# Attention values with V stationary and probabilities moving, turned output, and sums of squares by a matmul, in a float32 decoder layer

## The chip, the cores and the metric

The kernel runs on one core of a Trainium2 chip. It is one launch. The metric is the device time of one execution in microseconds (us). The engines are TensorE (PE; its weight loads are listed as PEld), VectorE (DVE), ScalarE (ACT), GpSimd (POOL) and SyncE (SP), which issues most DMAs.

## The reference

One pre-norm decoder layer on x of 256 x 1024, float32. Sixteen heads of 64: the first eight (group 0) are mixer A, causal attention (with 256 positions there is one block, so the block selection falls away); the last eight (group 1) are mixer B, a mixture of three dilated windows, which is one softmax with the log of a position's multiplicity added as a mask. What is computed, cut to what matters:

```python
qkv = jnp.einsum('bsd,de->bse', rmsnorm(x, attn_norm), w_in)
q, k = rope(q), rope(k)
p = softmax(q @ k.T * ATTN_SCALE + mask[group])     # per head
o = p @ v                                            # per head, 64 wide
o_g = rmsnorm(o of group g, 512 wide, gain_g)        # g = 0, 1
x = x + concat(o_0, o_1) @ w_out
h = rmsnorm(x, ffn_norm)
x = x + (silu(h @ w_gate) * (h @ w_up)) @ w_down
return rmsnorm(x, final_norm)
```

## The kernel before

All large matmuls run in three passes: activations and weights are split into a high part (written as fp32r by ACT) and a rest (DVE), and `three_pass` (L403 to L405) adds hi x hi, hi x lo and lo x hi in PSUM. The weights come as blocks of 128 x 512 through a ring of 12 (`raw`, `w_hi`, `w_lo`): SP loads four at a time (`ring_quad`), ACT splits pairs (L636), DVE makes the rest (L831), PE uses them. Blocks 0 to 47 are the q, k and v projections (six outputs in the order of `QKV_ORDER`, eight blocks each, six matmuls per block), 48 to 63 the output projection (four blocks at a time, first for rows 0 to 127, s = 0, then for s = 1), the rest the FFN, of which a loop does most.

Attention is laid between the blocks. Three tables, `PE_PLAN`, `DVE_PLAN` and `ACT_PLAN`, say behind (PE) or before (DVE, ACT) which block number an engine does which item; each engine takes its queue strictly in that order, so an item that waits holds what stands behind it. DVE's and ACT's splits stand in the same queues, behind the items of an odd number. On the items, with g the group and s or half the half of the rows:

- `rope` on DVE, in `rope_a`, `rope_b` and `rot`; `turn` transposes q or k on PE, ACT and DVE split it.
- `score(g, u)`: PE computes the scores of two tiles of 512 columns, the heads of even number on rows 0 to 63 of the array and those of odd number on rows 64 to 127 (L451 to L456), into banks 4 and 5; DVE adds the mask and takes the maxima; ACT does the exponentials with their sums (L720). u = 0 holds the first 128 queries of all eight heads, with 128 keys; u = 1 and 2 the other queries of four heads each, with 256 keys.
- `squares(g, t)`: DVE transposes the probabilities of tile t in squares of 32 (L921); SP places the squares by 4 DMAs into `landed` (`place_probs`, L368); `place` on ACT copies `landed` into `probsT` with its columns in order (L738).
- `values(g, t)`: PE, with a head's transposed probabilities stationary (128 x 128) and the head's 64 columns of `vals` moving, into bank 7 (L471), queries on the partitions.
- `norm`: DVE takes the reciprocal of the sums (L928) and multiplies bank 7 by it into `o_sb` (L931). `oturn`: PE transposes `o_sb` into bank 6 (L481); ACT squares `o_sb` with an accumulated sum (L667) and writes `o_hi` from bank 6 with the gain (L730); `olo` on DVE writes the rest (L941).
- `residual` on DVE adds a finished half of the output projection, scaled by rstd, which POOL makes for each group and half from the sum of squares.

## Time and profile before

| What | us |
|---|---|
| Median of 3 runs | 311.64 (311.19 to 312.02) |
| The profiled execution | 311.84 |
| Its span in the trace | 309.9 |
| PE busy, share of the span | 301.3, 97% |
| DVE busy | 200.7, 65% |
| ACT busy | 170.8, 55% |
| POOL busy | 10.3, 3% |
| DMA, mean share of 16 engines | 56.2% weights, placings and the like |

The span is what the trace covers; what lies around it is 1.9 us. Matmuls are pipelined and overlap in the records, so one that is listed with 390 ns comes every 230 ns; the distance of starts, or the pieces of the chain, tell what an instruction costs the engine. A float32 matmul appears as two instructions, an fp32r one as one. A group's mean is taken over its records.

### The profile page before, as it was taken

How to read it: one execution, taken by the hardware profiler on the slowest of the kernel's cores; microseconds unless marked ns; L12 is line 12 of the kernel's file. 1: busy time of each engine (PE TensorE's matmuls, PEld its weight loads, DVE VectorE, ACT ScalarE, POOL GpSimd, SP SyncE). 2: the span in 40 equal slices, each digit the busy share in tenths (PEclk: the TensorE clock that was granted, in tenths of full speed). 3: DMA queues.
4: the chain of work that ended last, by engine and by line, in shares of the span. 5: the costliest groups of instructions: out<-in, count | busy, mean ns of one | idle time of the engine just before them, and what ended most of it. 6: DMA issues, size and time to landing. Idle time of an engine off the chain costs nothing.

```text
span 309.9 us, 4293 instructions
## 1 busy us (share of the span) xinstructions
PE 301.3 (97%) x1430; PEld 246.1 (79%) x1430; DVE 200.7 (65%) x323; ACT 170.8 (55%) x294; POOL 10.3 (3%) x24
## 2 busy tenths in 40 slices
PE   7999999999999999999999999999999999999991
PEld 3788877788888988888888888888888888888880
DVE  3677979997877388855757374656565555555425
ACT  4785563968678458746453443526354444444224
POOL 0001000000020020200000000000000000000002
PEclk9999999999999999999999999999999999999998
DMA  6997635568482355482985656565657474561003
GB/s 200 390 410 298 222 111 161 189 185 286 116 285 71 144 170 237 153 316 78 347 326 170 224 183 210 187 223 176 252 170 270 161 256 174 209 220 31 0 0 135
DMA packets 22332, 61.59 MB, mean 199 GB/s; under 512 B 2608, under 2 KB 14000, under 8 KB 16432
## 3 DMA queue, kind: packets, MB, share of 16 engines
q1 hardware_dynamic: 22032, 60.89, 56.2%
q10 hardware_dynamic: 288, 0.54, 0.5%
q8 instruction: 7, 0.11, 0.1%
q14 instruction: 5, 0.04, 0.0%
HBM read 54.60 MB, written 1.05 MB: 180 GB/s over the span
## 4 chain that ended last, share of the span: by engine, by line
PE 96%; DMA 1%; ACT 1%; DVE 0%; POOLq 0%; issue 0%; POOL 0%
PE bank L403 30%; PE bank L404 29%; PE bank L405 29%; PE bank L471 3%; PE bank L430 2%; DMA gain<-in_gains 1%; PE bank L451 1%; PE bank L481 1%; PE bank L454 1%; PE bank L413 1%; PE bank L455 0%; PE bank L456 0%; POOLq L193 0%; ACT junk L667 0%; ACT rot L811 0%; DVE w_lo L851 0%
## 5 line engine op out<-in xcount | busy, mean ns | idle before, releaser
L636 ACT ACTIVATE w_hi<-raw 128x1024 fp32r<-128x1024 f32 x94 | 97.9, 1057 | 81.8 <-PE bank L405 71.9
L831 DVE TENSOR_TENSOR w_lo<-raw,w_hi 128x1024 fp32r<-128x1024 f32 x94 | 111.8, 1214 | 18.8 <-ACT w_hi L636 17.3
L403 PE MATMUL bank<-w_hi,x_hi 128*128 128x512 f32 x272 | 109.0, 401 | 0.8 <-DVE w_lo L851 0.8
L404 PE MATMUL bank<-w_lo,x_hi 128*128 128x512 f32 x272 | 106.6, 392 | 0.0
L405 PE MATMUL bank<-w_hi,x_lo 128*128 128x512 f32 x272 | 106.5, 392 | 0.0
L403 PEld LDWEIGHTS bank<-w_hi,x_hi 128*128 128x128 f32 x272 | 51.5, 189 | 13.1 <-DVE w_lo L851 2.2
L405 PEld LDWEIGHTS bank<-w_hi,x_lo 128*128 128x128 f32 x272 | 51.5, 189 | 11.1
L404 PEld LDWEIGHTS bank<-w_lo,x_hi 128*128 128x128 f32 x272 | 51.6, 190 | 10.1
L403 PE MATMUL bank<-w_hi,h_hi 128*128 128x512 f32 x80 | 31.2, 390 | 0.0
L405 PE MATMUL bank<-w_hi,h_lo 128*128 128x512 f32 x80 | 31.1, 389 | 0.0
L404 PE MATMUL bank<-w_lo,h_hi 128*128 128x512 f32 x80 | 31.1, 389 | 0.0
L969 DVE SCALAR_TENSOR_TENSOR rope_a<-bank,rstd,rope_b 128x256 f32<-128x256 f32 x22 | 9.8, 480 | 30.3 <-ACT rope_b L762 30.3
L983 DVE TENSOR_TENSOR h_lo<-landed,h_hi 128x512 fp32r<-128x512 f32 x10 | 6.9, 692 | 23.3 <-ACT h_hi L767 23.3
L720 ACT ACTIVATE probs<-probs,neg_max 128x128 f32<-128x128 f32 (+1 forms) x32 | 14.2, 444 | 8.3 <-DVE neg_max L910 8.3
L405 PEld LDWEIGHTS bank<-w_hi,h_lo 128*128 128x128 f32 x80 | 15.0, 188 | 3.1
L403 PEld LDWEIGHTS bank<-w_hi,h_hi 128*128 128x128 f32 x80 | 15.0, 188 | 3.1
L404 PEld LDWEIGHTS bank<-w_lo,h_hi 128*128 128x128 f32 x80 | 15.0, 188 | 3.0
L403 PE MATMUL bank<-w_hi,o_hi 128*128 128x512 f32 x40 | 16.3, 408 | 0.0
L405 PE MATMUL bank<-w_hi,o_lo 128*128 128x512 f32 x40 | 15.7, 392 | 0.0
L404 PE MATMUL bank<-w_lo,o_hi 128*128 128x512 f32 x40 | 15.6, 389 | 0.0
L762 ACT ACTIVATE rope_b<-bank,rstd 128x256 f32<-128x256 f32 x22 | 9.6, 465 | 4.1 <-PE bank L405 4.1
L471 PEld LDWEIGHTS bank<-vals,probsT 128*128 128x128 f32 x96 | 11.5, 192 | 0.4
(75 smaller groups left out, 233.9 us busy)
## 6 DMA issues: line engine op xcount, KB each, us to landing
raw<-in_weights SPq DMA_DIRECT2D x46, 1024.0 KB, 4.8
landed<-p_squares SPq DMA_DIRECT2D x88, 64.0 KB, 2.1
raw<-in_weights SPq DMA_DIRECT2D x5, 512.0 KB, 9.1
o_sb<-in_x_turned SPq DMA_DIRECT2D x4, 256.0 KB, 7.0
xs<-in_x SPq DMA_DIRECT2D x2, 512.0 KB, 8.5
out<-rot SPq DMA_DIRECT2D x4, 256.0 KB, 2.0
raw<-in_weights SPq DMA_DIRECT2D x2, 256.0 KB, 4.1
vals<-in_final_norm ACTq DMA_DIRECT2D x1, 512.0 KB, 7.2
```

Source lines behind the costliest of these rows:

```text
L403: pe.matmul(dst, a_hi, w1, start=first, stop=False)
L404: pe.matmul(dst, a_hi, w2, start=False, stop=False)
L405: return pe.matmul(dst, a_lo, w1, start=False, stop=last)
L413: ins = pe.transpose(dst[:, a * SEQ + s * P:a * SEQ + (s + 1) * P], xs[:, s, kt * P:(kt + 1) * P], ident)
L430: ins = pe.transpose(bank[TURN_BANK[qk_i][s]][:, p * P:(p + 1) * P], rot[:, qk_i, s, p * P:(p + 1) * P], ident_ja if qk_i else ident)
L471: ins = pe.matmul(bank[7][:, head * HEAD_DIM:(head + 1) * HEAD_DIM], probsT[:, T % PT_SLOTS, at:at + P], vals[:, g, b, head * HEAD_DIM:(he ...
L636: act.activation(w_hi[:, slot:slot + 2, :], raw[:, slot:slot + 2, :], ACT.Copy).then_inc(hi_ready, 1)
L720: ins = act.activation(piece, piece, ACT.Exp, bias=neg_max[:, g, half, head:head + 1], scale=-1.0, accum_out=sums[:, g, half, head:head + 1])
L762: act.activation(silu[:, s, :], bank[4 + s][:, 0:FC], ACT.Silu, scale=rstd[:, 6 + s:7 + s]).then_inc(silu_done, 1)
L831: dve.tensor_tensor(w_lo[:, slot:slot + 2, :], raw[:, slot:slot + 2, :], w_hi[:, slot:slot + 2, :].bitcast(f32), ALU.subtract).then_inc(lo ...
L969: dve.scalar_tensor_tensor(hid[:, s, :], bank[4 + s][:, FC:2 * FC], rstd[:, 6 + s:7 + s], silu[:, s, :], ALU.mult, ALU.mult).then_inc(hid_ ...
L983: dve.tensor_tensor(hidden[1], placed, hidden[0].bitcast(f32), ALU.subtract).then_inc(ht_lo, 1)
```

## The change

The values matmuls trade operands. Stationary is now a head's 128 x 64 of `vals`; moving are the 128 columns of its transposed probabilities, read straight from `landed` (four runs of 32 columns). Heads of even number go to the lower 64 columns of the array and lower 64 partitions of bank 7, those of odd number to the upper, alternately. So o comes out transposed, with (head, d) on the partitions and queries in the columns; `place` and `probsT` go, `landed` has 6 slots instead of 3, and three `values` items of 16 instructions stand for each group.

The reciprocal sums now must be transposed too: POOL widens them to 64 columns per head (`widen_rsums`, 512 columns, into `rope_a` or `rope_b`), PE transposes them (`rsum`) and ACT copies them to SBUF, all before `norm`, which multiplies the two. `oturn` goes; `o_hi` and `o_lo` are made from `o_sb`. Since the features are now on partitions, ACT squares `o_sb` (without a sum), POOL adds the four pieces of 128 columns (`add_squares`), and PE sums over the partitions by a matmul with a column of ones (`osum`), once for both halves of a group; DVE scales it, POOL makes rstd, one per group. The reciprocals are a DVE item of their own. The three tables and SP's places (`PLACE`) are written anew; of them two places stand below.

PE, before, from the block ahead of score(1, 0) on (L451 score, L471 values, L454 score(1, 1), L481 oturn; a row with x3 repeats the one above it):

```order
L451 MATMUL bank<-qkT_first 128x128 [waits max_ready,qk_lo,qk_first]
...
L471 MATMUL bank<-vals,probsT 128x64 [waits v_taken,p_placed]
L471 MATMUL bank<-vals,probsT 128x64 x3
L471 MATMUL bank<-vals,probsT 128x64 [waits p_placed]
...
L454 MATMUL bank<-qkT_hi 128x256 [waits max_ready,qk_lo]
...
L481 MATMUL bank<-tab,o_sb 128x128 [waits qk_lo,o_ready]
...
L471 MATMUL bank<-vals,probsT 128x64 [waits o_ready,p_placed]
```

The same stretch now (L461 score, L487 values, L464 score(1, 1)):

```order
L461 MATMUL bank<-qkT_first 128x128 [waits max_ready,qk_lo,qk_first]
...
L487 MATMUL bank<-landed,vals 64x128 [waits v_taken,rsum_taken,in_p1,in_p0]
L487 MATMUL bank<-landed,vals 64x128 x7
...
L464 MATMUL bank<-qkT_hi 128x256 [waits max_ready,qk_lo]
...
L487 MATMUL bank<-landed,vals 64x128 [waits o_ready,in_p3,in_p2]
...
L487 MATMUL bank<-landed,vals 64x128 [waits in_p5,in_p4]
```

Two `values` items of four matmuls have become one of eight before score(1, 1); the next comes right behind that score and waits for `o_ready`, which the first norm gives; the third stands alone.

ACT, before, from the placings ahead of the exponentials of score(1, 0) to the first o (L698 take, L711 turn, L720 exponentials, L667 and L730 o):

```order
L738 ACTIVATE probsT<-landed 128x512 [waits in_p1]
...
L698 ACTIVATE vals<-bank,rstd 128x512 [waits rstd_ready,blk_done]
...
L711 ACTIVATE qkT_hi<-bank 128x4x128 [waits scored,turned]
L636 ACTIVATE w_hi<-raw 128x1024 [waits blk_done,raw_full0]
L720 ACTIVATE probs,sums<-probs,neg_max 128x128 [waits max_ready]
...
L738 ACTIVATE probsT<-landed 128x512 [waits valued,in_p0]
...
L667 ACTIVATE junk,ssq<-o_sb 128x512 [waits sq_done,o_ready]
L730 ACTIVATE o_hi<-bank,gain 128x128 [waits b6_full]
```

The same stretch now (L738 turn, L756 copy of turned sums, L725 take, L663 splits, L747 exponentials, L763 and L769 o):

```order
L738 ACTIVATE qkT_hi<-qkT_first 128x4x128 [waits qk_first]
L756 ACTIVATE rot<-bank 128x512 [waits turned,rsum_turned]
L738 ACTIVATE qkT_hi<-bank 128x4x128 [waits scored,turned]
L725 ACTIVATE vals<-bank,rstd 128x512 [waits rstd_ready,blk_done]
...
L663 ACTIVATE w_hi<-raw 128x1024 [waits blk_done,raw_full0] x2
L747 ACTIVATE probs,sums<-probs,neg_max 128x128 [waits max_ready]
...
L763 ACTIVATE o_hi<-o_sb,gain 128x128 [waits o_ready]
...
L769 ACTIVATE rot<-o_sb 128x512 [waits turned]
```

The placings are gone, the second copy of turned sums stands ahead of the last turn, one more split stands ahead of the exponentials, and o follows directly on score(1, 0) with its squares last.

The diff, cut to what is spoken of:

```diff
+RSUM_BANK = 7, 6
...
-LANDINGS, PT_SLOTS = 3, 6
+SQUARES, LANDINGS = 3, 6
...
-    41: [("values", 0, 0), ("values", 0, 1)],
-    42: [("score", 1, 1), ("oturn", 0, 0)],
...
+    41: [("values", 0, 0)],
+    43: [("score", 1, 1), ("values", 0, 1)],
...
+        rsums_wide = rope_a, rope_b
+
+        rsums_turned = rot[:, 0, :, :]
+        o_squares, o_halves = rot[:, 1, 0, :], rot[:, 1, 1, 0:SEQ]
+        o_sums = rot[:, 1, 1, SEQ:GW].rearrange("p (s t) -> p s t", s=SH)
...
-                    sp.wait_ge(p_placed, T - LANDINGS + 1)
+                    sp.wait_ge(valued, (T - LANDINGS) // 2 + 1)
                 for i in range(JS):
                     sp.dma_start(landed[:, T % LANDINGS, i, :],
-                                 p_squares[i * SQ:(i + 1) * SQ, T % LANDINGS, :, :]).then_inc(in_p[T % LANDINGS], 16)
+                                 p_squares[i * SQ:(i + 1) * SQ, T % SQUARES, :, :]).then_inc(in_p[T % LANDINGS], 16)
...
                 elif kind == "values":
-                    _, g, t = it
-                    T = g * SC_TILES + t
-                    half, heads, keys = attention_tile(t)
-                    pe.wait_ge(p_placed, T + 1)
-                    if t == 0:
+                    _, g, u = it
+                    half, _, keys = attention_tile(2 * u)
+                    for r in range(2):
+                        T = g * SC_TILES + 2 * u + r
+                        pe.wait_ge(in_p[T % LANDINGS], (T // LANDINGS + 1) * 16 * JS)
+                    if u == 0:
                         pe.wait_ge(v_taken, 2 * g + 2)
-                    if t in (0, 2) and T:
+                        pe.wait_ge(rsum_taken, 2)
+                    if u in (0, 1) and g + u:
                         pe.wait_ge(o_ready, g * 2 + half)
                     kb = keys // P
-                    for i, head in enumerate(heads):
+
+                    for i in range(NB // keys):
                         for b in range(kb):
-                            at = (i * kb + b) * P
-                            ins = pe.matmul(bank[7][:, head * HEAD_DIM:(head + 1) * HEAD_DIM],
-                                            probsT[:, T % PT_SLOTS, at:at + P],
-                                            vals[:, g, b, head * HEAD_DIM:(head + 1) * HEAD_DIM],
-                                            start=(b == 0), stop=(b == kb - 1))
+                            for r in range(2):
+                                T, head = g * SC_TILES + 2 * u + r, attention_tile(2 * u + r)[1][i]
+                                x = i * kb + b
+                                dst = bank[7][64 * r:64 * r + 64, head // 2 * P:(head // 2 + 1) * P]
+                                ins = pe.matmul(dst.rearrange("p (i b) -> p i b", b=SQ),
+                                                vals[:, g, b, head * HEAD_DIM:(head + 1) * HEAD_DIM],
+                                                landed[:, T % LANDINGS, :, x * SQ:(x + 1) * SQ],
+                                                start=(b == 0), stop=(b == kb - 1))
                     ins.then_inc(valued, 1)
-                elif kind == "oturn":
+                elif kind == "rsum":
                     _, g, s = it
-                    pe.wait_ge(o_ready, g * 2 + s + 1)
-                    pe.wait_ge(*((ot_lo, g * 2 + s) if g * 2 + s else (qk_lo, 8)))
-                    for k in range(KT // 2):
-                        ins = pe.transpose(bank[6][:, k * P:(k + 1) * P], o_sb[:, g, s, k * P:(k + 1) * P], ident)
-                    ins.then_inc(b6_full, 1)
+                    n = g * 2 + s
+                    pe.wait_ge(rsum_wide, n + 1)
+                    if n:
+                        pe.wait_ge(rsum_taken, n)
+                    if n == 2:
+                        pe.wait_ge(qk_lo, 8)
+                    for p in range(HPAIRS):
+                        ins = pe.transpose(bank[RSUM_BANK[g]][:, p * P:(p + 1) * P], rsums_wide[s][:, p * P:(p + 1) * P], ident)
+                    ins.then_inc(rsum_turned, 1)
+                elif kind == "osum":
+                    g = it[1]
+                    pe.wait_ge(o_added, g * 2 + 2)
+                    pe.wait_ge(*((o_msq, 1) if g else (max_ready, 2 * SC_TILES)))
+                    for s in range(SH):
+                        ins = pe.matmul(bank[5][:, s:s + 1], o_sums[:, s, :], ones[:, 0:1], start=True, stop=True)
+                    ins.then_inc(o_summed, 1)
...
-                elif kind == "oturn":
+                elif kind == "rsum":
+                    _, g, s = it
+                    act.wait_ge(rsum_turned, g * 2 + s + 1)
+                    act.wait_ge(turned, 6)
+                    if g:
+                        act.wait_ge(o_ready, s + 1)
+                    act.activation(rsums_turned[:, s, :], bank[RSUM_BANK[g]][:], ACT.Copy).then_inc(rsum_taken, 1)
+                elif kind == "o":
                     _, g, s = it
                     n = g * 2 + s
-                    sum_squares(o_sb[:, g, s, :], GW, ssq[:, 2 + n:3 + n])
-                    act.wait_ge(b6_full, n + 1)
+                    act.wait_ge(o_ready, n + 1)
                     for k in range(KT // 2):
                         col = G_MIX + 4 * g + k
-                        ins = act.activation(o_hi[:, g * 4 + k, s * P:(s + 1) * P], bank[6][:, k * P:(k + 1) * P],
+                        ins = act.activation(o_hi[:, g * 4 + k, s * P:(s + 1) * P], o_sb[:, g, s, k * P:(k + 1) * P],
                                              ACT.Copy, scale=gain[:, col:col + 1])
                     ins.then_inc(ot_hi, 1)
-                elif kind == "place":
-                    T = it[1] * SC_TILES + it[2]
-                    act.wait_ge(in_p[T % LANDINGS], (T // LANDINGS + 1) * 16 * JS)
-                    if T >= PT_SLOTS:
-                        act.wait_ge(valued, T - PT_SLOTS + 1)
-                    act.activation(probsT[:, T % PT_SLOTS, :].rearrange("p (x i b) -> p x i b", i=JS, b=SQ),
-                                   landed[:, T % LANDINGS, :, :].rearrange("p i (x b) -> p x i b", b=SQ),
-                                   ACT.Copy).then_inc(p_placed, 1)
+                    if n:
+                        act.wait_ge(o_added, n)
+                    act.wait_ge(turned, 8)
+                    act.activation(o_squares, o_sb[:, g, s, :], ACT.Square).then_inc(o_squared, 1)
...
+                elif kind == "rsum":
+                    _, g, half = it
+                    dve.wait_ge(exp_done, g * SC_TILES + (SC_TILES if half else 2))
+                    dve.reciprocal(rsums[:, g, half, :], sums[:, g, half, :]).then_inc(rsum_ready, 1)
                 elif kind == "norm":
                     _, g, half = it
-                    t = SC_TILES - 1 if half else 1
                     n = g * 2 + half
-                    dve.wait_ge(exp_done, g * SC_TILES + t + 1)
-                    dve.reciprocal(rsums[:, g, half, :], sums[:, g, half, :]).then_inc(rsum_ready, 1)
-                    dve.wait_ge(valued, g * SC_TILES + t + 1)
-                    dve.wait_ge(rsum_ready, n + 1)
-                    dve.tensor_tensor(o_sb[:, g, half, :].rearrange("p (h d) -> p h d", h=GH),
-                                      bank[7][:].rearrange("p (h d) -> p h d", h=GH),
-                                      rsums[:, g, half, :].unsqueeze(2).to_broadcast([P, GH, HEAD_DIM]),
+                    dve.wait_ge(rsum_taken, n + 1)
+                    dve.wait_ge(valued, g * 3 + (3 if half else 1))
+                    dve.tensor_tensor(o_sb[:, g, half, :], bank[7][:], rsums_turned[:, half, :],
                                       ALU.mult).then_inc(o_ready, 1)
+                elif kind == "osum":
+                    g = it[1]
+                    dve.wait_ge(o_summed, g + 1)
+                    dve.tensor_scalar(msq[:, 2 + 2 * g:4 + 2 * g], bank[5][:, 0:SH], 1.0 / GW, EPS, ALU.mult,
+                                      ALU.add).then_inc(o_msq, 1)
...
-                        dve.wait_ge(rstd_ready, rstd_count[f"o{g}{s}"])
+                        dve.wait_ge(rstd_ready, rstd_count[f"o{g}"])
...
+            def add_squares(n):
+                pool.wait_ge(o_squared, n + 1)
+                if n >= 2:
+                    pool.wait_ge(o_summed, 1)
+                link(pool.tensor_tensor(o_halves, o_squares[:, 0:SEQ], o_squares[:, SEQ:GW], ALU.add))
+                pool.tensor_tensor(o_sums[:, n % 2, :], o_halves[:, 0:P], o_halves[:, P:SEQ],
+                                   ALU.add).then_inc(o_added, 1)
+
+            def inverse_rms_of_o(g):
+                c = slice(2 + 2 * g, 4 + 2 * g)
+                pool.wait_ge(o_msq, g + 1)
+                pool.tensor_tensor(rstd[:, c], msq[:, c], neg_half[:, c], ALU.pow).then_inc(rstd_ready, 1)
+
+            def widen_rsums(n):
+                g, s = n // 2, n % 2
+                pool.wait_ge(rsum_ready, n + 1)
+                pool.wait_ge(*((rsum_turned, n - 1) if g else (rotated, 8)))
+                pool.tensor_copy(rsums_wide[s][:].rearrange("p (h d) -> p h d", h=GH),
+                                 rsums[:, g, s, :].unsqueeze(2).to_broadcast([P, GH, HEAD_DIM])).then_inc(rsum_wide, 1)
+
+            widen_rsums(0)
+            widen_rsums(1)
+            widen_rsums(2)
+            add_squares(0)
+            add_squares(1)
+            widen_rsums(3)
+            inverse_rms_of_o(0)
+            add_squares(2)
+            add_squares(3)
+            inverse_rms_of_o(1)
+            inverse_rms_of_parts((6, 8), 4, 6)
```

## Rows read from the trace of the kernel before

**Rows 1.** The page: busy time by engine; the chain that ended last, by engine.
```profile
PE 301.3 (97%) x1430; PEld 246.1 (79%) x1430; DVE 200.7 (65%) x323; ACT 170.8 (55%) x294; POOL 10.3 (3%) x24
...
PE 96%; DMA 1%; ACT 1%; DVE 0%; POOLq 0%; issue 0%; POOL 0%
```

**Rows 2.** Waits of PE: who waited for whom, total us, times, longest.
```profile
PE bank L529 <- DVE warm L826: 1.2, 1, 1.2
PE bank L403 <- DVE w_lo L851: 0.8, 1, 0.8
```

**Rows 3.** Busy time by stretch: length, PE, PEld, DVE, ACT, POOL, clock, DMA, GB/s.
```profile
60.00:115.00 55.00, 55.00 (x323) 46.26 (x322) 41.29 (x92) 39.63 (x92) 4.58 (x8) 1.00 0.56 181
```

**Rows 4.** The chain in order of time: start us, us, what.
```profile
57.28 0.63 PE bank L430 x4
...
67.93 0.92 PE bank L430 x4
...
73.89 1.09 PE bank L451 x16
74.99 0.43 PE bank L403
75.42 0.23 PE bank L404
...
76.57 1.73 PE bank L471 x16
78.31 0.29 PE bank L403
...
79.75 0.32 PE bank L454 x2
80.66 0.59 PE bank L481 x4
...
82.63 3.52 PE bank L471 x32
...
90.33 0.44 PE bank L481 x4
...
94.66 0.84 PE bank L471 x8
```

**Rows 5.** Timeline of PE and its weight loads: start us, us, engine, line, operation.
```profile
73.82 1.16 PE L451 MATMUL bank<-qkT_first 64*128 64x128 f32 x16
...
76.41 1.89 PE L471 MATMUL bank<-vals,probsT 128*128 128x64 f32 x16
...
76.18 1.98 PEld L471 LDWEIGHTS bank<-vals,probsT 128*128 128x128 f32 x16
```

**Rows 6.** Groups by line and shape: busy us, mean ns | idle before.
```profile
L720 ACT ACTIVATE probs<-probs,neg_max 128x128 f32<-128x128 f32 x16 | 6.2, 389 | 1.1 <-DVE neg_max L910 1.1
...
L451 PE MATMUL bank<-qkT_first 64*128 64x128 f32 x32 | 2.3, 285 | 0.0
```

**Rows 7.** Timeline of ACT ahead of the exponentials of score(1,0).
```profile
72.05 1.25 ACT L698 ACTIVATE vals<-bank,rstd 128x512 f32<-128x512 f32 x2
73.19 0.59 ACT L711 ACTIVATE qkT_hi<-bank 128x512 fp32r<-128x512 f32 x1
74.94 1.06 ACT L636 ACTIVATE w_hi<-raw 128x1024 fp32r<-128x1024 f32 x1 [1.16 <-DMA raw<-in_weights]
```

**Rows 8.** Timeline of DVE: end of the last rope; squares(1,0) and norm(0,0).
```profile
68.15 0.69 DVE L874 TENSOR_TENSOR rot<-rope_a,rope_b 128x512 f32<-128x512 f32 x1
...
78.47 0.70 DVE L921 STREAM_TRANSPOSE p_squares<-probs 128x512 f32<-128x512 f32 x1
...
79.36 0.69 DVE L931 TENSOR_TENSOR o_sb<-bank,rsums 128x512 f32<-128x512 f32 x1
```

**Rows 9.** Timeline of POOL (its longest instruction) and of SP's queue (one placing).
```profile
109.17 1.44 POOL L1055 TENSOR_TENSOR rstd<-msq,neg_half 128x1 f32<-128x1 f32 x1
...
79.20 2.49 SPq L368 DMA_DIRECT2D landed<-p_squares  x4
```

170 lines of the change are left out of this document (87 added, 83 removed).

## Prediction

> **What bounds the kernel now.** First the page [rows 1]: TensorE (PE) is busy for 97% of the 309.9 us span, and 96% of the chain that ended last is PE's. Next whom PE waits for [rows 2]: the whole list is 1.2 + 0.8 us, both before the first weights are split. In the stretch where the values of attention are computed, 60 to 115 us [rows 3], PE is busy for all 55 us, at a granted clock of 1.00, the upper of its two levels. So two things can move the end: how long PE's own instructions take, and any wait that the change brings before one of them. The other engines have room: of the 55 us ACT is busy for 39.6, DVE for 41.3, POOL for 4.6 [rows 3].
>
> I price each thing that PE does between projections as its piece in the chain plus what the next weight matmul (L403) takes above its usual 0.23 us [rows 4].
>
> **Part 1, the values: -3.00 us.** Removed are the 96 L471 instructions (48 matmuls; each float32 matmul runs as two). In the chain they are five pieces, 1.73, 3.52 twice and 0.84 twice, 10.45 us, and the L403 behind each takes 0.05 or 0.06 too much (0.29 at 78.31): 10.74 us [rows 4]. What sets their pace? 16 in 1.73 us is 0.108 us each, and the x32 piece gives 0.110. They move only 64 columns. The L481 transposes move 128 columns in the same time, 0.44 us for 4 [rows 4], so two of these L471 should fit in it if columns were the limit. What both have in common is a load of 128 x 128 [rows 5]: it is the load that paces them.
>
> Added are 96 instructions as well, six items of 16: stationary is now 128 x 64 of vals, moving are 128 columns of landed, alternately into the lower and the upper 64 partitions of bank 7. Ends of their price: if the two halves of the array do not work side by side, each instruction moves 128 columns in 0.11 us (L481), and an item is 1.76 us before any extra for changing over. If they do, the nearest row is L451: also 16 instructions, float32, 128 moving columns, two heads alternately on two halves of the array (there rows 0-63 and 64-127, here columns). It takes 1.09 us, plus 0.20 in the L403 behind it: 1.29 us [rows 4]. Its own pace is 0.058 us each (1.16 us from first start to last end [rows 5], less the 0.285 us that one lasts [rows 6], over 15 steps), about half of 0.11; the rest, some 0.35 us, is paid once per item for going into and out of halves. A load of half as many columns should take half of 0.11, so that two fit beneath one pair's 0.117. I take L451's value, since kind, count, width and alternation agree: 6 x 1.29 = 7.74, and 10.74 - 7.74 = 3.00 us saved. Ends kept: 6 x 1.2 = 7.2 (3.5 saved) and 6 x (16 x 0.11 + 0.35) = 12.7 (2.0 lost).
>
> Do loads run beneath matmuls at all? The L471 rows say so, for matmuls on the very same rows of the array: 16 loads fill 1.98 us from 76.18 on, and 16 matmuls 1.89 us from 76.41 on [rows 5], where one after the other they would need the sum. The Trainium skill, "TensorE: Matmul & The Clock Gate", section "The mechanism", says that a weight load overlaps with matmuls in flight only when its row group differs, and two column halves share all row groups; by it the six items would lose what is priced as rival A, where the rows alone would save 3.0 us.
>
> **Part 2, transposes: 0.** Four items of four o transposes (L481: 0.44 us each, 0.59 beside a score [rows 4]) go; four items of four transposes of the widened inverse sums come, same shape. 4 x 0.44 against 3 x 0.44 + 0.59 is at most 0.15 less; I count nothing.
>
> **Part 3, sums of squares by PE: +0.95 us.** Two items of two float32 matmuls with one moving column: 8 instructions that load 128 x 128. With so few columns the load sets the pace, so L471 is the row: 8 of them are 0.84 + 0.05 us [rows 4], with a little for the second item's edge 0.95. Below it cannot fall much, loads of 128 being what they are; above, 0.35 us per item if narrow matmuls cost like a changeover: 0.9 to 1.6.
>
> **Part 4, the plan: -0.2 us.** The first turn of the second group is 0.63 us in the chain at 57.28, where four transposes of that form cost 0.44 (90.33) [rows 4]: it stands one block behind the score whose maxima it waits for. It now stands three blocks later. Scores and other turns keep number and shape.
>
> **Part 5, waits that could open.** I walked the new order by the old durations; a weight block on PE is 6 x 0.23 = 1.38 us.
> (a) ACT loses 12 placings and gains 4 copies of turned sums, all of 512 columns, so its total falls; o's squares stay, without the 4 readouts. (b) The tightest place: PE's second values item (behind block 43) overwrites bank 7 and waits for o_ready, so for DVE's first norm, and that now stands behind squares(1,0), squares(1,1), hence behind all eight exponentials of score(1,0). Count from the end of that score on PE. ACT's queue in front of the exponentials starts with the copy of the sums that PE turned 1.38 + 1.29 us earlier: the copy about 0.6 (like the turn), turn 0.59, take 1.25, two weight splits of 1.06 [rows 7], is 4.5, so ACT is free at +1.8; eight exponentials of 0.39 [rows 6]: +4.9; transpose, reciprocal and norm took DVE from 78.47 to 80.05 [rows 8], 1.6: +6.5. PE: three blocks 4.1, values 1.29, score(1,1) 0.91 (79.75 to 80.66) + 0.20 [rows 4]: +6.5. A tie. I count +0.15 us; here any lateness of ACT is paid in full by PE, and behind it in the queues stand only later scores and splits, which lead PE by microseconds (the pair for blocks 46 and 47 is split before it). (c) PE's rsum(0,0) waits for POOL to widen the sums, which waits for the last rope on DVE. That ended at 68.8 [rows 8]; a DVE turn and its wait for ACT no longer stand ahead of it, a short reciprocal does, and the walk has it at 67.6. PE comes there after the turn that the chain has at 67.93 for 0.92 us [rows 4], one block later and 0.2 us early: 70.0. So 1.2 us of room by the old time, 2.4 by the walk. No row shows POOL on 512 elements; its dearest instruction is 1.44 us [rows 9], DVE's 128 x 512 take 0.7 [rows 8]. I take 1.3, which the walk's room covers: no cost; at 4 us PE would wait 1.6 us once. (d) rstd for o now comes late: osum on PE, msq on DVE, then POOL; DVE's residual(0) waits with olo(1,0) behind it, which PE needs for block 56. In the walk olo(1,0) ends at 105.8 and PE comes at 108.5: 2.7 us of room, again POOL's. (e) SP: each placing holds its queue for 2.5 us [rows 9], and quads stand behind. Quad (4,1) now goes out behind placing 6, at about 83, and lands near 88; PE needs it at 100. Covered.
>
> The Trainium skill, "GPSIMD Engine Reference", section 3.1, gives a two-input add on POOL 1.96 times DVE's time; 0.7 us would become an estimated 1.4, inside the room in (c) and (d). No row here shows it, and the sum would not change.
>
> **Sum.** -3.00 + 0 + 0.95 - 0.2 + 0.15 = -2.1 us, all on PE. Nothing takes it back later: PE waits for nobody up to the last matmul [rows 2], and the quads that feed it leave SP no later than before. The profiled execution took 311.84 us (span 309.9): 309.7. The median, 311.64, gives 309.5; I say 309.6, and count the rivals from the same middle, 311.7.
>
> **Rivals.**
> A, slower: the halves take turns. Then an item is 16 x 0.11 + 0.35 = 2.1 us instead of 1.29, six are 12.7, and the sum is 1.9 + 0.9 = +2.8: 314.5 us. For: two streams now read the same 128 partitions, where L451's read 64 each. Against: at 128 columns in 0.11 us float32 moves at half the pace of the main matmuls (512 in 0.23 us [rows 4]), which leaves room for a second stream. The end turns to slower from an item of 1.64 us on, (10.74 - 0.9) / 6. A second way into the same place: the loads of the halves do not run beneath matmuls but stand bare, 2 x 0.055 us on top of each pair's 0.117. That makes 8 x 0.23 + 0.35 = 2.2 us an item, +3.3 in all, 315.0 us; as loads do run beneath matmuls in [rows 5] it gets 3 of A's 13 in 100. The rule of the Trainium skill named in part 1 would bring it about.
> B, about the same: the halves overlap, but place (b), (c) or (d) opens by 1 to 2 us. ACT a microsecond behind the walk, or POOL at 4 us or more for 512 elements, would do. Sum -1.1 to -0.1: 311.1 us. Against: all places but one have over 2 us of room.
> C, partly: a pair costs 0.16 to 0.18 us (a load of 64 columns dearer than half of one of 128): an item 1.6 to 1.8, sum -0.1 to +0.9: 312.1 us.
> D, the change frees more than counted (items at 1.2 or under, no tie): sum -2.9: 308.8 us.
>
> **Chances.** Forecast (308.9 to 310.6) 58, B 16, A 13, C 8, D 5 in 100. The range takes in the forecast, D, B and the lower edge of C: 308.4 to 312.0; it leaves out A and most of C. A measurement of this kernel can tell about 0.3%, 0.94 us, from no change. Faster by more: the forecast, D and a quarter of B, 0.67. Within: the rest of B, and C, 0.20. Slower: A, 0.13.
>
> **What would show it.** Values items of 1.1 us in the chain, 16 instructions each at 0.06 us: part 1 right; at 0.11: A. The L403 behind them near 0.43. Two pieces of 0.4 to 0.5 us for the sums. A PE wait on DVE's norm ahead of the second values item: (b), its length the error of the walk. A wait on ACT's copy near 70 or on ot_lo near 106: POOL, with its 128 x 512 copies over 2.3 us. PE busy for all but 2 us of the span up to 301 would mean that nothing was given back.

## The result

| | median, us | lowest to highest |
|---|---|---|
| Kernel before | 311.8 (4 runs) | 311.19 to 312.02 |
| Changed kernel | 308.99 (4 runs) | 308.27 to 309.37 |

The ratio is 0.991, 95% interval 0.9887 to 0.9934: faster by 0.9%, 2.8 us. Timed once more on another chip beside a fresh set of runs of the kernel before, it gave 309.26 us against 311.68, 0.9914 [0.9898, 0.9930]. The prediction was 309.6 us. One execution in all that follows, of runs_contiguous, took 430.8 us at a mean granted clock of 0.66 and is slow; no ratio counts it.

**The profile after.** The profiled execution took 309.37 us, its span is 307.5 us. Busy time by engine, and the chain that ended last, by engine (against [rows 1]):

```profile
PE 297.4 (97%) x1438; PEld 239.8 (78%) x1438; DVE 201.7 (66%) x325; ACT 166.8 (54%) x282; POOL 18.4 (6%) x31
...
PE 93%; DMA 3%; SPq 1%; ACT 1%; DVE 0%; POOLq 0%; issue 0%; POOL 0%
```

PE's busy time fell by 3.9 us, POOL's rose by 8.1. Whom PE waits for: in total us, times, longest (against [rows 2]):

```profile
PE bank L413 <- DVE w_lo L878: 2.5, 3, 1.4
PE bank L556 <- DVE warm L853: 1.2, 1, 1.2
```

All four of these stands end by 14.2 us, at the start of the kernel, while the first weights are being split; in the second profiled execution of the changed kernel they are 2.3 and 1.2 us. No wait on a norm, on ACT's `o_hi` or on a placed tile has come in. The attention stretch (against [rows 3]; columns: length, PE, PEld, DVE, ACT, POOL, clock, DMA, GB/s) says the same: PE is busy for all of it.

```profile
60.00:115.00 55.00, 55.00 (x347) 43.36 (x347) 42.96 (x94) 37.62 (x82) 12.72 (x14) 1.00 0.55 183
```

The chain in order of time (start us, us, what), with the rows that answer to [rows 4]:

```profile
60.44 0.44 PE bank L440 x4
...
70.48 0.44 PE bank L501 x4
...
75.05 1.09 PE bank L461 x16
76.15 0.43 PE bank L413
...
77.73 1.02 PE bank L487 x16
78.76 0.43 PE bank L413
...
82.65 1.02 PE bank L487 x16
...
98.93 0.34 PE bank L508 x4
99.27 0.35 PE bank L413
```

A values item is 1.02 us in the chain with 0.20 to 0.23 us in the L413 behind it; before, its 16 instructions took 1.73 (L471). What each item adds to the distance between the starts of the weight matmuls around it gives a full account (a weight matmul counted with 0.2285 us):

| us on PE | before | after | difference | predicted |
|---|---|---|---|---|
| values, all | 10.79 | 7.27 | -3.52 | -3.00 |
| first turn of group 1 | 0.69 | 0.45 | -0.24 | -0.2 |
| transposes of o; of the widened sums | 1.77 | 1.77 | 0 | 0 |
| sums of squares by PE | - | 0.92 | +0.92 | +0.95 |
| second values item waiting for a norm | - | 0 | 0 | +0.15 |
| all items of attention and the FFN's turns | 27.17 | 24.36 | -2.81 | -2.1 |

Of the six values items five cost 1.24 to 1.26 us each, and the one directly behind score(1, 1) 1.02.

The span fell by 2.4 us only. In this execution PE's first turn came at 30.66 us against 30.19 before, 0.47 later, ahead of everything that the change touches; in the second profiled execution of the changed kernel it came at 30.21, and there the span is 307.1 us, 2.8 less than before.

### The profile page after: what moved, and what is told of

Same layout as the page of the kernel before. It is cut to its first block, busy times and chain, and to the rows that moved or that the text cites. A ratio compares the mean times of both kernels' runs of the same rounds, so it can differ in the third digit from the quotient of the medians.

```text
span 307.5 us, 4312 instructions
## 1 busy us (share of the span) xinstructions
PE 297.4 (97%) x1438; PEld 239.8 (78%) x1438; DVE 201.7 (66%) x325; ACT 166.8 (54%) x282; POOL 18.4 (6%) x31
## 4 chain that ended last, share of the span: by engine, by line
PE 93%; DMA 3%; SPq 1%; ACT 1%; DVE 0%; POOLq 0%; issue 0%; POOL 0%
PE bank L413 29%; PE bank L415 28%; PE bank L414 28%; DMA raw<-in_weights 3%; PE bank L487 2%; PE bank L440 2%; PE bank L461 1%; PE bank L464 1%; PE bank L501 1%; PE bank L423 1%; SPq L344 0%; SPq L334 0%; PE bank L465 0%; POOLq L192 0%; PE bank L466 0%; ACT junk L694 0%
## 5 line engine op out<-in xcount | busy, mean ns | idle before, releaser
L663 ACT ACTIVATE w_hi<-raw 128x1024 fp32r<-128x1024 f32 x94 | 97.9, 1056 | 82.4 <-PE bank L415 72.4
L858 DVE TENSOR_TENSOR w_lo<-raw,w_hi 128x1024 fp32r<-128x1024 f32 x94 | 112.0, 1217 | 17.4 <-ACT w_hi L663 16.2
L413 PE MATMUL bank<-w_hi,x_hi 128*128 128x512 f32 x272 | 108.2, 398 | 2.5 <-DVE w_lo L878 2.5
L413 PEld LDWEIGHTS bank<-w_hi,x_hi 128*128 128x128 f32 x272 | 51.1, 188 | 15.6 <-DVE w_lo L878 4.2
L413 PE MATMUL bank<-w_hi,h_hi 128*128 128x512 f32 x80 | 31.2, 390 | 0.0
L747 ACT ACTIVATE probs<-probs,neg_max 128x128 f32<-128x128 f32 (+1 forms) x32 | 14.1, 448 | 6.2 <-DVE neg_max L937 6.2
L413 PEld LDWEIGHTS bank<-w_hi,h_hi 128*128 128x128 f32 x80 | 15.0, 188 | 3.1
L413 PE MATMUL bank<-w_hi,o_hi 128*128 128x512 f32 x40 | 16.4, 410 | 0.0
```

The source lines that it names most:

```text
L413: pe.matmul(dst, a_hi, w1, start=first, stop=False)
L663: act.activation(w_hi[:, slot:slot + 2, :], raw[:, slot:slot + 2, :], ACT.Copy).then_inc(hi_ready, 1)
L747: ins = act.activation(piece, piece, ACT.Exp, bias=neg_max[:, g, half, head:head + 1], scale=-1.0, accum_out=sums[:, g, half, head:head + 1])
L858: dve.tensor_tensor(w_lo[:, slot:slot + 2, :], raw[:, slot:slot + 2, :], w_hi[:, slot:slot + 2, :].bitcast(f32), ALU.subtract).then_inc(lo ...
```

## Experiments

The open questions after the result: whether the two halves of the array really work side by side, and what sets the pace; what a visit to the halves costs once, whatever stands in it; how near the waits were that did not come; and where the sums' 0.92 us comes from. "Changed kernel" stands for the 308.99 us (309.26 in the last set).

**halves_in_turn.** Do the halves overlap at all, or are the instructions only short?

```diff
-                    for i in range(NB // keys):
-                        for b in range(kb):
-                            for r in range(2):
+                    for r in range(2):
+                        for i in range(NB // keys):
+                            for b in range(kb):
```

> The changed kernel with one difference: within a values item the eight matmuls of the lower half of the array come first, then the eight of the upper half, instead of alternately. Same instructions, same loads of 64 columns. Theory 1 (the gain of the values comes from two halves at work at the same time): the 16 instructions of an item run at 0.11 us each, as the transposes of 128 columns do, except where the halves meet; an item costs about 1.9 to 2.1 us instead of 1.21, so six add 4.1 to 5.3 us: 313 to 314.5 us. Theory 2 (the gain comes from loads of half the width, and the halves do not matter): the items stay at 1.0 us in the chain and the time at 309.0.

(The eight on each half are instructions; they belong to four matmuls.)

Measured: 311.93 us, ratio 1.0005 [0.9991, 1.0019]: the whole gain is gone. That is less than the 313 to 314.5 us of theory 1, and far from theory 2's 309.0. The chain, and PE's timeline, of an item:

```profile
77.38 1.51 PE bank L487 x16
```
```profile
77.31 1.58 PE L487 MATMUL bank<-landed,vals 128*64 128x128 f32 x16
```

An item costs 1.73 us instead of 1.25 (1.50 behind a score instead of 1.02); 6 x 0.48 = 2.9, which is the difference of the times. The same instructions, in another order: the gain of the change lies in the alternation of the halves. But 1.73 is also less than rival A's 2.1.

**one_half.** Rival A's price itself: in turn, and all in the lower half.

```diff
-                                dst = bank[7][64 * r:64 * r + 64, head // 2 * P:(head // 2 + 1) * P]
+                                dst = bank[7][0:64, head // 2 * P:(head // 2 + 1) * P]
```

> As halves_in_turn, but both sets of eight matmuls go to the lower half of the array and the lower 64 partitions of bank 7 (so the upper heads of o are left wrong). Nothing can run side by side now, while loads stay at 64 columns. Theory 1 (two halves at work at once make the gain; where they met in halves_in_turn about four instructions still ran beside others): 16 x 0.11 us, an item of 1.73 to 2.0 us in all, against 1.21 alternating: +3.1 to +4.7, 312.1 to 313.7 us. Theory 2 (halves_in_turn lost time for another reason than lost overlap): the same 311.9 as there or less.

Measured: 313.94 us, 1.0071 [1.0054, 1.0087]. In the chain:

```profile
77.07 1.89 PE bank L487 x16
```

An item costs 2.10 us, what rival A was priced at (16 x 0.11 + 0.35). Against it halves_in_turn saves 0.38 us per item, where its order meets the other half once: some 3.5 instructions of 0.11 us. That is how far the second half's matmuls ran beside the first half's; it isn't far enough for eight instructions to run beside eight.

The first moments of an item show the two halves directly. PE's timeline of the changed kernel, cut to 77.60 to 77.90 us, and of one_half, cut to 76.95 to 77.20:

```profile
77.66 0.44 PE L487 MATMUL bank<-landed,vals 128*64 128x128 f32 x4
```
```profile
77.00 0.43 PE L487 MATMUL bank<-landed,vals 128*64 128x128 f32 x2
```

In the same time four instructions run alternately and two on one half. In the single records of the changed kernel they start in pairs, under 0.01 us apart, and the pairs come 0.109 us apart behind the first; in one_half single instructions come 0.109 us apart. So each half keeps the pace it has alone, and the 0.0545 us of an alternating instruction is two such streams.

**runs_contiguous.** The moving operand is read as four runs of 32 columns. Does that cost?

```diff
-                                ins = pe.matmul(dst.rearrange("p (i b) -> p i b", b=SQ),
+                                ins = pe.matmul(dst,
...
-                                                landed[:, T % LANDINGS, :, x * SQ:(x + 1) * SQ],
+                                                landed[:, T % LANDINGS, x, :],
```

> The changed kernel, but the values matmuls read 128 contiguous columns of a landed tile instead of four runs of 32 (so they multiply columns in the wrong order; o is left wrong, all else is computed from it as it comes). Theory 1 (runs of 32 columns cost PE nothing): 309.0, item pieces of 1.02. Theory 2 (each jump costs something): pieces under 1.0; with 3 jumps of about 5 ns in each of 96 instructions on two halves up to -0.7 us, 308.3.

Measured: 309.06 us over three executions (309.23 with the fourth, of 430.8), 0.9914 [0.9894, 0.9933], with items of 1.24 and 1.26 us as in the changed kernel. The runs of 32 cost nothing on PE that these items show; the 5 ns per jump of theory 2 was assumed, and no run shows it.

**before_32.** What paced the values before? The kernel before, moving half as many columns:

```diff
-                            ins = pe.matmul(bank[7][:, head * HEAD_DIM:(head + 1) * HEAD_DIM],
+                            ins = pe.matmul(bank[7][:, head * HEAD_DIM:head * HEAD_DIM + 32],
...
-                                            vals[:, g, b, head * HEAD_DIM:(head + 1) * HEAD_DIM],
+                                            vals[:, g, b, head * HEAD_DIM:head * HEAD_DIM + 32],
```

> The kernel before, with values matmuls that move 32 columns per head instead of 64 (half of o is left wrong); the stationary probabilities stay 128 x 128. Theory 1 (the load of 128 columns sets the pace, 0.108 us): pieces of 1.73 and 3.52 as before, the time unchanged, 311.9. Theory 2 (moving columns set it): the pieces shrink by a third or more, -3 us or more.

Measured: 312.05 us, 1.0022 [1.0005, 1.0039]; the five values pieces cost 1.81, 3.58, 0.90, 0.90 and 3.59 us, as before. Six of the ten executions took 311.60 to 312.12 us, at a mean granted clock of 0.994 or 0.995, and four 313.14 to 313.91 at 0.989 to 0.991, which lifts the ratio; the profiled one is of the six, and what the clock did in the four is not recorded in a trace. The chain's first:

```profile
76.26 1.71 PE bank L471 x16
```

The moving columns did not pace it: 0.107 us each at 32 columns as at 64. That leaves the load of 128 x 128, or a least time per instruction of the same length; these runs don't tell the two apart, since none of them has a narrow load and few moving columns on the same half.

**items_joined.** A visit to the halves should cost something once. Two pairs of items are put side by side:

```diff
-    43: [("score", 1, 1), ("values", 0, 1)],
-    45: [("values", 0, 2)],
+    43: [("score", 1, 1), ("values", 0, 1), ("values", 0, 2)],
...
-    52: [("values", 1, 1)],
...
-    54: [("values", 1, 2)],
+    54: [("values", 1, 1), ("values", 1, 2)],
```

> The changed kernel with two values items of each group moved so that they follow each other on PE: (0, 2) directly behind (0, 1) at block 43, and (1, 1) directly ahead of (1, 2) at block 54. In the changed kernel a values item between weight matmuls costs 1.25 us, and the one that directly follows a score 1.02. Theory 1 (0.23 us are paid for each way into and out of halves, not for each item): two such ways fewer, -0.46 us, 308.5. Theory 2 (each item pays): 309.0. Theory 3: the moved items wait (for placed tiles or for the norm): PE stands for up to 1 us and the time is 309.5 to 310.

Measured: 308.54 us, 0.9894 [0.9877, 0.9910]. The items' total is 23.92 us, 0.44 less than in the changed kernel. In the chain:

```profile
81.94 1.90 PE bank L485 x32
...
102.91 1.02 PE bank L485 x16
103.93 0.02 issue
103.95 1.09 PE bank L485 x16
```

The first pair costs 1.89 us behind its score (after 1.02 + 1.24 = 2.26): the second item is 0.87 us, 16 x 0.054. The second pair broke in two, and costs 2.36; PE's list names no wait for it, but joined_fp32r and joined_placed below point to the second item's placed tile. So 1.25 us of a lone item are 0.87 of work and 0.38 of going in and out; directly behind a score, which is in halves already, 0.15 is left of the 0.38. The time is theory 1's 308.5.

**act_later.** The tie of step (b) came out as no wait. How much room was there? One ACT copy of 1024 columns stands ahead of the exponentials of score(1, 0):

```diff
+        act_pad = sb("act_pad", [P, D_MODEL], bf16)
...
+                    if (g, u) == (1, 0):
+                        act.activation(act_pad[:], tab[:, 0:D_MODEL], ACT.Copy)
```

> The changed kernel with one copy of 1024 columns more on ACT (1.05 us, into a buffer nobody reads), directly ahead of the exponentials of score(1, 0). In the changed kernel DVE's first norm ended 0.37 us before PE reached the values item that waits for it. Theory 1 (that place is the tight one and has 0.4 us of room, beyond which PE pays in full): PE waits about 0.65 us ahead of its second values item, 309.6 to 309.7. Theory 2 (other work covers it): 309.0 and no wait of PE.

Measured: 309.94 us, 0.9937 [0.9921, 0.9954]. PE's waits, and its timeline:

```profile
PE bank L488 <- DVE o_sb L962: 0.7, 1, 0.7
```
```profile
83.16 1.09 PE L488 MATMUL bank<-landed,vals 128*64 128x128 f32 x16 [0.72 <-DVE o_sb L962]
```

In the changed kernel the norm (L959) ends at 81.64 + 0.64 = 82.28 and the values start at 82.65: 0.37 us of room. The copy took 1.07 us; 1.07 - 0.37 = 0.70, and 0.72 is what PE waited. The place of (b) and the chain ACT, DVE, PE through it are as described, and lateness is paid in full: the items' total is 0.8 us above the changed kernel's.

**pool_later.** The same for (c): three POOL copies of 512 columns stand ahead of the first widening.

```diff
+        pool_pad = sb("pool_pad", [P, 3, NB])
...
+                for _ in range(3 if n == 0 else 0):
+                    pool.tensor_copy(pool_pad[:, _, :], tab[:, 0:NB])
```

> The changed kernel with three more POOL copies of 512 columns (into a buffer nobody reads) ahead of the first widening of the sums. In the changed kernel a widening took 1.47 and 1.50 us while DVE subtracted 128 x 1024 (w_lo), and 0.62 and 0.61 us while it did not; the first ended at 69.0, PE came for it at 70.5. Theory 1 (POOL and DVE's two-input reads from SBUF hold each other up): the added copies last 0.6 to 1.5 each depending on what DVE does beside them, DVE's subtractions near them take 1.4 instead of 1.2, and PE waits 1 to 3 us for the sums: 310 to 312 us. Theory 2 (POOL's first copies are slow by themselves): only the first copy lasts 1.5, the others 0.6, the sums come at about 70.9 and PE waits 0.4: 309.4.

Measured: 312.76 us, 1.0020 [1.0009, 1.0031], 3.8 us above the changed kernel and above the 310 to 312 expected. PE's waits:

```profile
PE bank L502 <- POOL rope_a L1124: 2.2, 1, 2.2
...
PE bank L488 <- DMA landed<-p_squares: 0.4, 1, 0.4
```

POOL's timeline, DVE's beside it, and the granted clock by stretch (seventh column; the columns are length, PE, PEld, DVE, ACT, POOL, clock, DMA, GB/s):

```profile
67.21 3.57 POOL L1123 COPY pool_pad<-tab 128x512 f32<-128x512 f32 x3 [42.82 <-DVE rot L902]
70.73 1.60 POOL L1124 COPY rope_a<-rsums 128x512 f32<-128x512 f32 x1
72.28 0.61 POOL L1124 COPY rope_b<-rsums 128x512 f32<-128x512 f32 x1
```
```profile
68.83 3.03 DVE L859 TENSOR_TENSOR w_lo<-raw,w_hi 128x1024 fp32r<-128x1024 f32 x2
```
```profile
70.00:73.00 3.00, 0.75 (x5) 0.61 (x5) 1.86 (x2) 0.00 (x0) 2.89 (x3) 0.93 0.90 333
73.00:76.00 3.00, 3.00 (x11) 2.55 (x10) 0.00 (x0) 2.59 (x4) 0.00 (x0) 0.50 0.07 22
76.00:80.00 4.00, 4.00 (x31) 3.13 (x31) 1.91 (x7) 3.10 (x6) 0.00 (x0) 1.00 0.00 0
```

PE stood for 2.2 us, and then for about 3 us worked at 0.50, the lower of its two levels (1.2 GHz). The weight matmuls in it show it in the chain:

```profile
74.24 0.43 PE bank L414
74.67 0.43 PE bank L415
75.10 0.43 PE bank L416
```

They cost 0.43 us instead of 0.23. The group of items around the wait cost 5.58 us instead of 2.29, 3.3 more for a wait of 2.2; the slow weight matmuls behind it add some 0.3 and the wait on a placed tile 0.4. That is 4.0 us in the profiled execution, which at 313.07 is on the long side of the ten.

The other executions weigh the clock by itself. Nine of the ten took 312.19 to 313.12 us, at a mean granted clock of 0.989 to 0.991; the tenth took 311.70, at 0.995. The tenth is 2.7 us above the changed kernel, about the two waits, 2.2 + 0.4, and no more. As far as one execution without a trace can tell, the waits themselves are paid one for one, and the fall of the clock, where it comes, adds an estimated 1.2 us (312.94, the median of the nine, less 311.70).

**joined_fp32r.** The sums of squares by PE cost 0.92 us for four float32 matmuls, eight instructions. On top of items_joined, they are fp32r, one instruction each:

```diff
+            pool.tensor_copy(ones_r[:], ones[:]).then_inc(consts_ready, 1)
...
-                pool.tensor_tensor(o_sums[:, n % 2, :], o_halves[:, 0:P], o_halves[:, P:SEQ],
+                pool.tensor_tensor(osums_r[:, n % 2, :], o_halves[:, 0:P], o_halves[:, P:SEQ],
...
-                        ins = pe.matmul(bank[5][:, s:s + 1], o_sums[:, s, :], ones[:, 0:1], start=True, stop=True)
+                        ins = pe.matmul(bank[5][:, 2 * s:2 * s + 2], osums_r[:, s, :], ones_r[:], start=True, stop=True)
```

> items_joined, and the sums of squares by PE with fp32r operands (POOL writes its second sum as fp32r, two columns of ones move): one instruction per matmul instead of two. Theory 1 (a narrow matmul costs what the load of its 128 columns costs): each osum item drops from 0.47 us to about 0.2 to 0.25, together -0.5 us against items_joined's 308.5: 308.1. Theory 2 (a fixed part dominates): no change against items_joined. Theory 3: POOL takes longer to write fp32r; no effect on the end, since its sums have microseconds of room.

Measured: 308.68 us, 0.9892 [0.9875, 0.9908], not the 308.1 of theory 1 and no less than items_joined's 308.54. The two sums cost 0.24 us each instead of 0.46, so 0.46 us were saved, and given back at once. PE's waits and the chain:

```profile
PE bank L487 <- DMA landed<-p_squares: 0.6, 1, 0.6
```
```profile
100.73 3.86 DMA landed<-p_squares
104.59 0.14 issue
104.73 1.09 PE bank L487 x16
```

The last tile's placing goes out behind a weight quad on SP and lands 0.6 us after PE is there. In the changed kernel it had been in time; PE now comes to it some 1 us sooner, by what it has gained up to there.

**joined_placed.** Both together, and the last placing ahead of the quad:

```diff
-PLACE = {(3, 0): (0,), (3, 1): (1,), (3, 2): (2, 3, 4, 5), (4, 0): (6,), (4, 1): (7,), (4, 2): (8,), (5, 0): (9, 10), (5, 1): (11,)}
+PLACE = {(3, 0): (0,), (3, 1): (1,), (3, 2): (2, 3, 4, 5), (4, 0): (6,), (4, 1): (7,), (4, 2): (8,), (5, 0): (9, 10, 11)}
```

> joined_fp32r, with the placing of the last tile issued by SP ahead of weight quad (5, 1) instead of behind it. In joined_fp32r PE stood 0.6 us for that tile, whose four placings took up to 3.9 us to land beside the quad's 1 MB. Theory 1 (the wait came from that order): no wait of PE for placed tiles, and the 0.46 us that the fp32r sums gave back come through: 0.6 us under joined_fp32r, about 308.1. Theory 2 (the quad, now later by 2 us, is late for the FFN's first blocks): PE waits for w_lo near 115 us and nothing is gained.

Measured: 307.76 us (307.69 to 308.21), 0.9873 [0.9855, 0.9891]: 3.9 us under the kernel before, 1.5 under the changed kernel, run beside it. SP's queue, and the chain:

```profile
89.76 10.64 SPq L378 DMA_DIRECT2D landed<-p_squares  x12
```
```profile
82.37 1.90 PE bank L487 x32
...
103.07 1.90 PE bank L487 x32
```

Both pairs are now whole (2.12 us for the lone one, 1.89 behind the score), the wait on a placed tile is gone, and the items total 23.18 us, 1.16 less than the 24.34 of the changed kernel beside it; the spans differ by 1.1 (306.0 and 307.1). This is the best version found.

**changed_again.** The changed kernel on that chip, for the comparison.

> The changed kernel once more, on the same chip as joined_placed: 309.0 us (308.7 to 309.4).

Measured: 309.26 us (308.76 to 309.31), 0.9914 [0.9898, 0.9930]; items 24.34 us in all. What the result said holds.

**pool_quiet.** POOL and DVE slowed each other in places. Does it reach the end? The first of POOL's two additions, of 256 columns, is left out:

```diff
-                link(pool.tensor_tensor(o_halves, o_squares[:, 0:SEQ], o_squares[:, SEQ:GW], ALU.add))
-                pool.tensor_tensor(o_sums[:, n % 2, :], o_halves[:, 0:P], o_halves[:, P:SEQ],
+                pool.tensor_tensor(o_sums[:, n % 2, :], o_squares[:, 0:P], o_squares[:, P:SEQ],
```

> The changed kernel without POOL's first addition (256 columns) of o's squares, so that only two of the four pieces of 128 columns go into the sums (rstd of o is left wrong). In the changed kernel DVE's four o_lo instructions take 1.63 us twice, exactly where that addition runs beside them, and 1.10 and 1.13 us elsewhere. Theory 1 (POOL's and DVE's reads of two SBUF operands hold each other up): all four groups take 1.1 us. Theory 2 (their operands in SBUF make them slower than before, whatever POOL does): 1.63 stays. Either way the end does not move, 309.0, since DVE has microseconds of room there.

Measured: 309.05 us, 0.9914 [0.9896, 0.9932], as changed_again. The o_lo instructions on DVE, in the changed kernel and then here with POOL's remaining addition beside them:

```profile
90.72 1.63 DVE L972 SCALAR_TENSOR_TENSOR o_lo<-o_sb,gain,o_hi 128x128 fp32r<-128x128 f32 x4 [1.13 <-ACT o_hi L763]
```
```profile
90.26 1.35 DVE L972 SCALAR_TENSOR_TENSOR o_lo<-o_sb,gain,o_hi 128x128 fp32r<-128x128 f32 x4 [1.20 <-ACT o_hi L763]
...
90.83 0.63 POOL L1108 TENSOR_TENSOR rot<-rot 128x128 f32<-128x128 f32 x1 [5.72 <-ACT rot L769]
```

POOL's addition beside it fell from 0.92 to 0.63 us and DVE's four fell by as much, 0.28, not to theory 1's 1.1, since one addition still stands there; where nothing of POOL stands beside them they take 1.10. It is a real hold-up, and it costs nothing here, since PE comes later than either.

**before_turn.** The part of the plan alone: in the kernel before, the first turn of group 1 stands with the second, one block further from the score.

```diff
-    30: [("turn", 1, 0, 0)],
-    31: [("turn", 1, 0, 1)],
+    31: [("turn", 1, 0, 0), ("turn", 1, 0, 1)],
```

> The kernel before, with the first turn of the second group behind block 31 instead of 30, directly ahead of its twin. Theory 1 (it cost 0.69 us instead of 0.45 because it waited for the maxima of the score one block ahead): it costs 0.45 there, -0.24 us. Theory 2 (the price belongs to the first transposes after a score): 0.69 again.

Measured, in one run: 311.66 us, span 309.6 (309.9 before). In the chain:

```profile
58.56 0.87 PE bank L429 x8
```

Both turns together cost 0.89 us, against 0.69 + 0.46: the 0.24 us of part 4 belong to the distance from the score and are won without the rest of the change. Whether it is the maxima, due later, or something else in the score's neighbourhood isn't shown. One run can't show 0.24 us in the time; the items do.

## Why the prediction was right, and where it was off

The direction, the cause and the place were right: the gain is PE's values matmuls (-3.52 us) and the moved turn (-0.24), less 0.92 for the sums; PE waits for nobody new, and nothing is given back later. From the first item on the change is worth 2.8 us where the sum said 2.1; the time, 308.99, lies just inside the forecast's range of 308.9 to 310.6.

**What bounds the kernel.** Holds: PE is busy for 55.00 of 55.00 us in the stretch after as before. Nothing but PE's own instructions, its waits and its clock moved the experiments' times: in act_later, pool_later and joined_fp32r every wait that was brought in showed there, and pool_quiet, which eased DVE and POOL alone, changed nothing.

**Part 1, right in kind and mis-sized.** The term was 6 x 1.29 = 7.74 us and measured 7.27. The choice of L451 as the analog was the step that mattered, and it was right; one_half put the other end at exactly its price. Two things inside the term were off. The pace: L487 runs at (1.09 - 0.273) / 15 = 0.0545 us from first start to last end, L451 at 0.058, so an item's work is 0.87 and not 0.93 us; the going in and out, 0.35 in the prediction, is 0.38 (items_joined). That is 0.04 us an item. And the plan puts one item directly behind a score: in and out is paid once for both, and 0.23 us are saved that I did not look for, though the order rows of the change showed it (values right behind score(1, 1)). Together -0.47; another 0.05 since the values cost 10.79 before and not 10.74. The step "it is the load that paces them" is half shown: before_32 excludes the columns, not a least time per instruction. On one half alone, loads of 64 columns with 128 moving ones came every 0.109 us as well (one_half). What makes the new pace is two such streams side by side; that it takes loads of half the width, as the prediction argued, no run tests.

Loads run beneath the matmuls here too. PE's timeline of one item and of its weight loads:

```profile
77.66 1.09 PE L487 MATMUL bank<-landed,vals 128*64 128x128 f32 x16
```
```profile
77.66 0.85 PEld L487 LDWEIGHTS bank<-landed,vals 128*64 128x64 f32 x16 [0.36 <-issue]
```

16 loads fill 0.85 us inside 1.09 us of matmuls; bare, they would have made an item 2.2 us. The rule weighed in the prediction (the Trainium skill, "TensorE: Matmul & The Clock Gate", section "The mechanism": a load overlaps only where the row group differs) doesn't hold in this trace, where both halves use all row groups; the measurement decides. The same section of the Trainium skill also lets a load into the background weight buffer go ahead; no run here tells whether that is what these loads do.

**Part 2, right.** The four transposes of o cost 1.77 us in all (0.39 to 0.46 each), the four of the widened sums 1.77 (0.41 to 0.46).

**Part 3, right.** 0.47 + 0.45 = 0.92 us against 0.95: with one moving column eight instructions cost 0.115 each, and joined_fp32r halves the instructions and the cost. Whether their loads or a least time per instruction make the 0.115 is as open as in part 1.

**Part 4, right.** -0.24 against -0.2, and before_turn shows it alone.

**Part 5.** (b) The tie of +0.15 was none. The walk put both at 6.5 us after the end of score(1, 0), at 76.15. PE's values did come at 82.65, +6.5. The norm ended at +6.1: ACT was free at 77.70, +1.55 and not +1.8, the rest as walked. act_later shows that the room is 0.37 us and that the mechanism is the one described. (c) The widening copies took 1.47 and 1.50 us, not 1.3, in POOL's timeline:

```profile
67.56 1.47 POOL L1121 COPY rope_a<-rsums 128x512 f32<-128x512 f32 x1 [42.47 <-DVE rot L901]
69.32 1.50 POOL L1121 COPY rope_b<-rsums 128x512 f32<-128x512 f32 x1 [0.30 <-DVE rsums L953]
81.78 0.62 POOL L1121 COPY rope_a<-rsums 128x512 f32<-128x512 f32 x1 [10.96 <-DVE rsums L953]
```

The text's room of 1.2 to 2.4 us runs from the last rope to PE and has yet to hold the copy. Measured, it is 3.1: the rope ended at 67.4, PE came at 70.48 (chain above). The first copy ended at 69.03 and left 1.45 of it. Undisturbed a copy takes 0.62 (third row); the guess was near for the wrong reason, as the first two stand beside DVE's splits. The sentence that at 4 us "PE would wait 1.6 us once" is where the prediction was wrong in kind: in nine of ten executions of pool_later the clock fell behind such a wait, and more than the wait was paid. Rival B was priced too low for that reason. (d) olo(1, 0) ended at 104.6 (walk 105.8), and PE came to block 56 at about 108 (walk 108.5). (e) Quad (4, 1) went out at 82.65 (walk 83); it was there at 88.45 (walk 88), where ACT took it.

**The rivals.** A didn't come, but what it describes exists: in another loop order (halves_in_turn) half of it comes back (1.73 us an item between 1.25 and 2.10) and the gain is nil. D came nearer than its 5 in 100 say: the items average 1.21 us and the tie was none, and 308.99 lies 0.2 us from D's 308.8 and 0.6 from the forecast's 309.6. The 0.7 us between 2.8 and 2.1 are 0.52 in the values (the pace too dear, the changeover a little too cheap, the item behind a score overlooked), 0.15 in the tie, and 0.07 in the moved turn and the sums. Nearly all lie on one side, and the result came within 0.1 us of leaving the range.

## What to carry to other kernels

Small stationary operands pay in pairs: alternate the two halves of the array matmul by matmul, since the same instructions half by half lost the whole gain here (1.73 against 1.25 us for 16), and put such items directly behind one another or behind other work in halves, for each way in and out costs 0.38 us. Before giving PE a new operand from an engine with a queue of its own, walk the order to the place where it is due and count the room; a wait of 2.2 us cost 3.3 and more where the clock fell behind it. A microsecond won on PE brings every transfer forward that PE waits for: look at which one is next before timing, as the last placing here ate 0.46 us that a move in SP's order gave back.

## What the hardware showed that I had not expected

- **How far the halves run apart.** In turn, 8 instructions on one half and 8 on the other overlap by 0.38 us only, about 3.5 instructions of 0.11 us (halves_in_turn against one_half), though nothing in the data orders them.
- **The clock behind a wait.** After PE stood 2.2 us, at full busy before and after, the granted clock was 0.50 (1.2 GHz) for the stretch 73 to 76 us, and 1.00 again in 76 to 80. It did not come every time: one of ten executions kept a mean of 0.995. Nor does it need such a wait: four executions of before_32 and one of halves_in_turn also show 0.989 to 0.991 and lie some 1.4 to 1.7 us above the others of their kernel, though no wait of this size was added to them and no trace shows where their clock fell. The nine executions of the changed kernel all lie at 0.993 or above. Behind act_later's 0.7 us there is no such stretch:

```profile
83.00:85.00 2.00, 1.84 (x20) 1.55 (x20) 2.00 (x10) 1.95 (x6) 0.21 (x2) 1.00 0.71 139
85.00:88.00 3.00, 3.00 (x26) 2.34 (x24) 2.39 (x6) 1.82 (x8) 1.58 (x2) 1.00 0.81 298
```

- **POOL and DVE hold each other up.** A copy of 0.62 us took 1.47 and 1.50 beside DVE's splits (L858), and the two splits took 2.72 us beside it where a pair in the kernel before took 2.35, and 3.03 in pool_later. The copy at 81.78 ran at its 0.62 although DVE was busy with the norm, which reads one operand from PSUM; the splits and L972 read both from SBUF. The Trainium skill, "SBUF — State Buffer", section "SBUF: two separate sides", says that a DVE operation with two SBUF inputs and a GpSimd operation that reads SBUF take a shared pair of ports in turn, the later one blocked until the first is done. The trace agrees: DVE's split from 67.33 gave way to its next instruction, which reads PSUM, at 68.47; the first copy, due from 67.56, ended at 69.03, and its own 0.62 us counted from 68.47 would give 69.09.
- **POOL's additions.** They took 0.73 us for 256 columns undisturbed and 0.46 for 128. For 512 columns the prediction had an estimated 1.4 us, from the factor of 1.96 over DVE in the Trainium skill, "GPSIMD Engine Reference", section 3.1. By the step of 0.27 per 128 columns the rows would put 512 at an estimated 1.3, close to it; no run here has such an addition.
